# Projection groups in another order: index rows and softmax values first, queries and keys second, with the indexer inside the second group

## The reference

```python
a = rmsnorm(h, g_attn)
qa, ka, va, qi, ki, wi, qb, kb, vb, u = split_columns(a @ w_in)
qa = rope(rmsnorm(qa.reshape(B, T, 6, 64), g_q_a), pos)
ka = rope(rmsnorm(ka.reshape(B, T, 2, 64), g_k_a), pos)
qi = rope(qi.reshape(B, T, 4, 64), pos)
ki = rope(ki[:, :, None, :], pos)[:, :, 0]
...
s_idx = einsum('bqhd,bsd->bqhs', qi, ki) * 64 ** -0.5
score = einsum('bqhs,bqh->bqs', relu(s_idx), wi)      # the indexer
_, sel = top_k(where(causal, score, -inf), topk)      # 128 of 512 keys
...                                                   # softmax attention over sel
z = einsum('bqhd,bshd->bhqs', qb, kb) * 64 ** -0.5     # stick-breaking attention
rev = cumsum(where(strict, log_sigmoid(-z), 0), axis=3, reverse=True)
o_b = exp(where(strict, z + rev, -inf)) @ vb
```

## Time and profile before

| | |
|---|---|
| median of 3 runs | 1616.64 us (1613.22 to 1617.04) |
| the profiled execution, its own time | 1620.47 us |
| its span in the profile | 1618.7 us |
| PE busy | 1556.1 us, 96% |
| DVE busy | 883.4 us, 55% |
| ACT busy | 683.5 us, 42% |
| POOL busy | 276.4 us, 17% |
| mean granted TensorE clock | 0.984 of full speed |

### The profile page before, as it was taken

One profiled execution on the slowest core, in us unless ns is written; L12 is line 12 of the kernel. 1 busy time (PEld: TensorE's weight loads), 2 busy tenths in 40 slices (PEclk: granted clock), 3 DMA queues, 4 the chain that ended last, 5 costly groups with the idle time before them and its releaser, 6 DMA issues.

```text
span 1618.7 us, 30649 instructions
## 1 busy us (share of the span) xinstructions
PE 1556.1 (96%) x11772; PEld 1415.8 (87%) x11772; DVE 883.4 (55%) x1534; ACT 683.5 (42%) x995; POOL 276.4 (17%) x474
## 2 busy tenths in 40 slices
PE   6999989999999999999999998899999999999998
PEld 5787746999999999999977776479999999999998
DVE  6668884245555553222857688624455555432345
ACT  4444556244444442224443444644444444322241
POOL 3420340111111110100115105202111111101000
PEclk8999999999999999999999999999999999999999
DMA  5233144123333233322222511332233323333221
GB/s 166 66 99 87 34 142 110 53 66 91 91 90 89 80 87 100 92 81 85 79 69 77 138 40 58 105 98 86 72 91 91 91 78 91 98 88 92 84 70 61
DMA packets 225719, 140.24 MB, mean 87 GB/s; under 512 B 13122, under 2 KB 219604, under 8 KB 225552
## 3 DMA queue, kind: packets, MB, share of 16 engines
q1 hardware_dynamic: 223220, 133.46, 28.3%
q0 software_dynamic: 2400, 5.42, 1.0%
HBM read 131.21 MB, written 7.65 MB: 86 GB/s over the span
## 4 chain that ended last, share of the span: by engine, by line
PE 79%; DVE 13%; ACT 3%; issue 3%; POOL 1%; DMA 0%; DVEq 0%; SPq 0%; ACTq 0%; POOLq 0%
PE ps L1714 23%; PE ps L1716 22%; PE ps L1715 22%; DVE score L1379 3%; DVE m L1376 3%; DVE w_L L1270 2%; PE ps L2065 1%; PE ps L1994 1%; DVE Lb L1451 1%; PE ps L1741 1%; PE ps L1797 1%; PE ps L1905 1%; PE ps L1767 1%; PE ps L2149 1%; PE ps L1907 1%
## 5 line engine op out<-in xcount | busy, mean ns | idle before, releaser
L1714 PE MATMUL ps<-bH,w_H 128*128 128x272 f32 x1664 | 481.1, 289 | 4.7 <-DVE w_L L1270 3.2
L1270 DVE TENSOR_TENSOR w_L<-w_raw,w_H 128x1024 fp32r<-128x1024 f32 (+4 forms) x236 | 257.6, 1100 | 414.1 <-ACT w_H L890 411.3
L1716 PE MATMUL ps<-bH,w_L 128*128 128x272 f32 x1664 | 479.6, 288 | 0.0
L1715 PE MATMUL ps<-bL,w_H 128*128 128x272 f32 x1664 | 477.9, 287 | 0.0
L890 ACT ACTIVATE w_H<-w_raw 128x1024 fp32r<-128x1024 f32 (+4 forms) x236 | 220.1, 943 | 270.1 <-PE ps L1716 269.4
L1714 PEld LDWEIGHTS ps<-bH,w_H 128*128 128x128 f32 x1664 | 312.6, 188 | 6.3 <-DVE w_L L1270 4.1
L1715 PEld LDWEIGHTS ps<-bL,w_H 128*128 128x128 f32 x1664 | 313.6, 188 | 0.1
L1716 PEld LDWEIGHTS ps<-bH,w_L 128*128 128x128 f32 x1664 | 312.6, 188 | 0.0
L1714 PE MATMUL ps<-actH,w_H 128*128 128x272 f32 x704 | 204.2, 290 | 0.0
L1716 PE MATMUL ps<-actH,w_L 128*128 128x272 f32 x704 | 203.8, 289 | 0.0
L1715 PE MATMUL ps<-actL,w_H 128*128 128x272 f32 x704 | 202.7, 288 | 0.0
(11 more groups left out here) (343 smaller groups left out, 2326.6 us busy)
## 6 DMA issues: line engine op xcount, KB each, us to landing
w_raw<-in_w_up SPq DMA_DIRECT2D x88, 512.0 KB, 3.7
w_raw<-in_w_down SPq DMA_DIRECT2D x32, 512.0 KB, 3.9
w_raw<-in_w_in SPq DMA_DIRECT2D x24, 512.0 KB, 5.0
w_raw<-in_w_ple_gate SPq DMA_DIRECT2D x16, 512.0 KB, 3.9
w_raw<-in_w_down SPq DMA_DIRECT2D x16, 384.0 KB, 3.4
w_raw<-in_w_out SPq DMA_DIRECT2D x16, 320.0 KB, 3.5
w_raw<-in_w_in SPq DMA_DIRECT2D x8, 452.0 KB, 4.0
w_raw<-in_w_in SPq DMA_DIRECT2D x8, 384.0 KB, 3.6
```

Of the source, the lines that this page charges most:

```text
L1270: ins = dve.tensor_tensor(w_L[u % SPLIT][:, a:b], w_raw[raw_slot(l, u)][:, a:b], w_H[u % SPLIT][:, a:b].bitcast(F32), ALU.subtract)
L1714: pe.matmul(out, wh, xh, start=start, stop=False)
L1715: pe.matmul(out, wh, xl, start=False, stop=False)
L1716: return pe.matmul(out, wl, xh, start=False, stop=stop)
```

## The change

`CHUNK` is turned around: group 0 is now softmax values, index queries, key and weights (452 columns), group 1 the softmax queries and keys (512). All that hangs on the order of the groups follows: the index rows are rotated first (`rope_ok` 1 to 5) and the queries and keys last (`rope_ok` 6 to 10), and `turn(0, ...)` now has three blocks and `turn(1, ...)` four. The six calls of TensorE's `index` move from between the products of units 12 to 14 into group 1, after `k` 4, 5 and 6 and in the middle of `k` 5, 6 and 7; their banks change, and the first two tiles of group 2 wait for the last relus. Both parts of `decode_step` stand after `k` 5 (before: after 3 and after 5). GpSimd multiplies the gains into the rotation's tables once (`rot_q`, `rot_k`, each cos and sin for five tiles), so a tile needs one product on GpSimd instead of three; the squares are made by ScalarE (`ACT.Square` in `leave(1, t)`), and VectorE only adds them up. Seven of the 16 rounds for the first tile run before the rotations of queries and keys, six more between units 13 and 15, three after `split(16)`. From `select(2, 13, 16)` on the lists are as they were. SP's list isn't edited.

```diff
-CHUNK = [(0, 512), (512, 964), (1732, 2116)]
+CHUNK = [(512, 964), (0, 512), (1732, 2116)]
...
-CH_BLOCKS = [(F_QA, 4), (F_QI, 3)]
+CH_BLOCKS = [(F_QI, 3), (F_QA, 4)]
...
-                pool.tensor_scalar(gains[:, 0, :], gains[:, 0, :], 0.125, None, ALU.mult)
-                pool.wait_ge(hs_rec, at(hs_rec, 1))
+                pool.tensor_scalar(gains[:, 0, :], gains[:, 0, :], 0.125, None, ALU.mult).then_inc(pool_step, steps.step())
...
+                for g, out in ((0, rot_q), (1, rot_k)):
+                    gn = gains[:, g, :].unsqueeze(1)
+                    cs, sn = (dcon[:, d:d + TILES * HD].rearrange("p (t d) -> p t d", d=HD) for d in (D_COS, D_SIN))
+                    pool.tensor_tensor(out[:, 0, :, :], cs, gn.to_broadcast([P, TILES, HD]), ALU.mult)
+                    for a in (0, 32):
+                        pool.tensor_tensor(out[:, 1, :, a:a + 32], sn[:, :, a:a + 32],
+                                           gn[:, :, 32 - a:64 - a].to_broadcast([P, TILES, 32]), ALU.mult)
...
+                pool.wait_ge(hs_rec, at(hs_rec, 1))
...
+                    pool.tensor_tensor(x, x, hstat[0:n, t, :].unsqueeze(2).to_broadcast([n, 8, HD]), ALU.mult).then_inc(qk_ok, 1)
...
                 part_copy(0)
-                for t in range(TILES):
+                leave(0, 0)
+                split(5)
+                for t in range(1, TILES):
                     leave(0, t)
...
                 split(6)
+                turned(0, 0)
+                turned(0, 1)
+                turned(0, 2)
                 split(7)
...
+                turned(0, 3)
+                turned(0, 4)
+                relu(1, 0, 4)
                 split(8)
                 part_copy(1)
...
+                relu(2, 0, 4)
+                relu(3, 0, 4)
+                leave(1, 0)
+                leave(1, 1)
                 split(9)
...
                 split(10)
-                turned(0, 4)
-                turned(1, 0)
+                act.wait_ge(hs_ss, at(hs_ss, 5))
+                inverse(hstat[:, :, :], hstat[:, :, :], 1.0 / HD).then_inc(hs_rec, 1)
                 split(11)
...
+                turned(1, 4)
+                split(16)
...
+                select(1, 4, 7)
+                split(11)
                 qk(0)
-                split(7)
                 qk(1)
-                split(8)
+                split(12)
                 qk(2)
                 qk(3)
-                split(9)
+                split(13)
                 qk(4)
...
                     if step:
-                        pe.wait_ge(w_lo, at(w_lo, RAW + 4 * c + 3 + 1))
+                        u = 4 * c + 3
+                        pe.wait_ge(w_ld[raw_slot(l, u)], ld_value(l, u))
...
+                            if c == 1 and t == 1:
+                                if k in (2, 4):
+                                    turn(0, 1 if k == 2 else 4)
+                                elif k > 4:
+                                    index(k - 4, 2)
-                        if k in (3, 5):
-                            decode_step(c, (k - 3) // 2)
+                        if k == 5:
+                            decode_step(c, 0)
+                            decode_step(c, 1)
...
+                        if c == 1 and k in (1, 2, 3):
+                            turn(0, (0, 2, 3)[k - 1])
+                        if c == 1 and k in (4, 5, 6):
+                            index(k - 3, 0)
+                turn(1, 0)
...
-                for t in range(1, 4):
+                for n in range(3):
                     for half in range(2):
-                        feature(t - 1, half, 0, 4)
...
+                        feature(n, half)
+                        if 2 * n + half < 4:
+                            turn(1, 2 * n + half + 1)
```

More of the change, by code:

```diff
@@ L382, in build @@
         F_BANK = [1, 3, 5, 6, 6, 6, 6, 6]
[L383 removed]
+        I_BANK = [3, 4]
         def act_at(of, f):
@@ L732, in _ @@
-                    pool.tensor_tensor(x[:, 6:8, :], x[:, 6:8, :], gains[0:n, 1, :].unsqueeze(1).to_broadcast([n, 2, HD]), ALU.mult).then_inc(qk_ok, 1)
-                for t in range(TILES):
+                    store("a_v", t, "n d", V[:, t, 0:128], kv_out)
                     pool.wait_ge(rope_ok, at(rope_ok, t + 1))
                     hold(pool)
[L736 to L742, removed]
@@ L743, in _ @@
                     store("idx_k", t, "d", r_tok[:, t, 256:320], ix_out)
[L744 to L747, removed]
                 for t in range(1, 4):
@@ L753, in _ @@
                                        pattern=[[-1, P]], channel_multiplier=1).then_inc(i_diag, 1)
+                pool.wait_ge(hs_rec, at(hs_rec, 1))
+                hold(pool)
+                for t in range(TILES):
+                    n = TOKW[t]
+                    pool.wait_ge(p_ev, at(p_ev, 5 + t + 1))
+                    x = x_tok[0:n, t, :].rearrange("p (h d) -> p h d", d=HD)
+                    pool.tensor_tensor(x, x, hstat[0:n, t, :].unsqueeze(2).to_broadcast([n, 8, HD]), ALU.mult).then_inc(qk_ok, 1)
+                for t in range(TILES):
+                    pool.wait_ge(rope_ok, at(rope_ok, 5 + t + 1))
+                    hold(pool)
+                    store("a_k", t, "n d", r_tok[:, t, 384:512], ak_out)
+                    pool.wait_ge(p_ev, at(p_ev, 10 + t + 1))
+                    hold(pool)
+                    store("b_v", t, "n d", V[:, t, 128:512], kv_out)
                 pool.memset(qim, 0.0).then_inc(d_zero, 1)
@@ L970, in leave @@
                             act.wait_ge(n_rec, at(n_rec, 1))
-                        ins = copy(x_tok[0:n, t, :], src, r)
+                        copy(V[0:n, t, 0:128], src[:, 0:128], r)
+                        ins = copy(x_tok[0:n, t, 0:324], src[:, 128:452], r)
                     elif c == 1:
-                        copy(V[0:n, t, 0:128], src[:, 0:128], r)
-                        act.wait_ge(rope_ok, at(rope_ok, t + 1))
-                        ins = copy(x_tok[0:n, t, 0:324], src[:, 128:452], r)
+                        act.wait_ge(rope_ok, at(rope_ok, 5 if t == 0 else t + 1))
+                        if t >= 2:
+                            act.wait_ge(hs_ss, at(hs_ss, t - 1))
+                        copy(x_tok[0:n, t, :], src, r)
+                        ins = act.activation((t1, t2)[t % 2][0:n, :], src, ACT.Square, scale=r)
                     else:
@@ L1027, in _ @@
                     leave(2, t)
-                for t in range(1, 4):
-                    relu(t, 0, 4)
-                    split(U_F + t + 1)
+                turned(1, 0)
+                turned(1, 1)
+                split(14)
+                turned(1, 2)
+                turned(1, 3)
+                split(15)
+                turned(1, 4)
+                split(16)
                 def stick_exp(h):
@@ L1341, in qk @@
                     dve.wait_ge(qk_ok, at(qk_ok, t + 1))
+                    dve.wait_ge(t_mm, at(t_mm, t + 1))
+                    dve.wait_ge(ix_out, at(ix_out, 5 * 16))
+                    hold(dve)
                     rotate(t, 8, [(r_tok[0:n, t, 0:384], 0, 384, True), (r_tok[0:n, t, 384:512], 384, 512, False)])
@@ L1831, in _ @@
                             square_sum(0)
-                        if c == 1 and k == 1:
+                        if c == 1 and k == 0:
                             pe.wait_ge(lay_ld, at(lay_ld, 6 * 16))
@@ L1868, in feature @@
                         mm.then_inc(w_used, 1)
-                for t in range(1, 4):
+                for n in range(3):
                     for half in range(2):
-                        feature(t - 1, half, 0, 4)
-                        if t > 1:
-                            index(t, 2 * half)
-                        elif half:
-                            index(1, 0)
-                        feature(t - 1, half, 4, KD)
-                    if t == 1:
-                        index(1, 2)
+                        feature(n, half)
+                        if 2 * n + half < 4:
+                            turn(1, 2 * n + half + 1)
                 def logits(q):
```

132 lines of the change are left out of this document (57 added, 75 removed).

## The result

| | before | after |
|---|---|---|
| median | 1616.84 us (4 runs, 1613.22 to 1617.38) | 1644.12 us (4 runs, 1643.49 to 1645.89) |
| ratio, 95% interval | | 1.0165 (1.0149 to 1.0182) |
| profiled execution, its span | 1620.47, 1618.7 us | 1644.15, 1642.4 us |
| mean granted clock | 0.984 | 0.979 |

The account below looks back on a forecast made before the run. TensorE, busy 96% of the span, was taken as the bound. Per layer 9.6 (later remainders) + 2.7 (clock) - 1.5 (fewer rounds) = 10.8, 21.6 for both; added to the 1616.6 median: 1638 us, range 1623 to 1648.

Parts of the forecast that it names:

- the mechanism: Later last rotation delays unit 16's load, so TensorE stands 11 us ahead of its first remainders; chance 0.60.
- Rival C: More waits among group 1's index calls make rotations and all behind 3 us later: +28 us, 1644; chance 0.09.
- the ladder: Group 1's chain of index call, relu, weighing and index call again: twelve rungs, each between k blocks of 2.8 us.
- Ahead of the logits: TensorE's stretch through unit 12, predicted to start at 107.6, up to the stick-breaking logits, predicted at 130.3.
- the lead of 1 us: TensorE reaching the stick-breaking logits at 130.3 instead of 131.32, with indexer products moved ahead of unit 12.
- Group 1: Old 2.93 us decode_step wait goes, a new 2.4 us one comes ahead of index(2, 2), halving the clock; net -0.5 us.
- rival B: Same late load, cheaper: group 1's pause keeps full clock, rotations earlier, no clock loss after the long pause; 1624 to 1629; chance 0.20.
- The old wait's cause: The 2.93 us in group 1: splits of units 6 and 7 stood behind rotations sharing time with GpSimd.
- The load: rope_ok is 10 at 115.0, 10.9 us later; unit 16 issues 20.8 us after, at 135.8, and lands at 139.7.
- Behind the load: After unit 16's splits, five VectorE rounds take 6.8 us to stick_max; first remainders at 150.3 against 140.73.
- The clock: Behind the long pause ahead of the first remainders, TensorE runs 5.4 us at half clock, losing 2.7 us.
- Behind that: After the half-clock stretch, seven fewer first-tile rounds behind split(16) relieve VectorE, removing a TensorE wait: -1.5 us.

Follow-up runs that it names:

- e1: Changed kernel, with SP loading units 16 and 17 ahead of the wait for the last rotation and the index-key pages: 1617.74 us, ratio 1.0009.
- e3: Kernel before, with SP also waiting, ahead of the index-key pages, until VectorE has copied out unit 12's product: 1633.24 us, ratio 1.0099.
- e5: Kernel before, with SP loading units 16 and 17 ahead of the wait for the last rotation: 1618.52 us, ratio 1.0002.
- e11: e6 with VectorE's split(12) moved between the first and second rotation of queries and keys: 1608.06 us, ratio 0.9944 to the kernel before.
- e6: e1 with the two parts of decode_step back after k 3 and k 5: 1611.24 us, ratio 0.9957 to the kernel before.
- e9: Kernel before, with only the tables rot_q and rot_k, so GpSimd has one product per tile instead of three: 1611.05 us, ratio 0.9963.
- e10: Kernel before, with only the second part of decode_step waiting on the landed load instead of VectorE's split: 1612.81 us, ratio 0.9970.
- e4: Changed kernel, with 45 extra bf16 products keeping TensorE busy in the pause ahead of the first remainders: 1641.60 us, ratio 1.0150 to the kernel before.
- e7: e1 with ScalarE's relu(2, 0, 2) ahead of split(8) and relu(2, 2, 4) behind part_copy(1): 1616.54 us, ratio 0.9991 to the kernel before.
- e12: Kernel before, with both the rotation tables and the second decode_step part's wait on the landed load: 1610.63 us, ratio 0.9954.

## Why the prediction was right, step by step

The forecast (1638, range 1623 to 1648, slower) named the mechanism, and e1, e3 and e5 show it. The measured time is 6 us above it: 2 us are in the table below, and 4 us come from the baseline, since the profiled execution of before lies above its median and that of the change doesn't. Rival C, more waits inside group 1, had named 1644, the very time measured, but its mechanism didn't come: in group 1 there is one wait, the one of the forecast, and e1 gives the time back without touching the ladder.

- **Ahead of the logits.** Logits predicted at 130.3, measured 130.52; but TensorE's first dense product also started 0.85 us earlier, so the lead of 1 us didn't come in layer 0. Two errors cancelled: unit 12 started at 108.9, not 107.6 (a wait of 1.54 that I had set at nothing, because `split(12)` stands behind two rotations, as e11 shows on e6, where 1.21 of it were left), and the stretch behind it was 1.1 us shorter, for a reason that wasn't looked for. That the logits came on the forecast is luck. Nor did group 0 stay without a new wait: TensorE stood there for 1.31 us in layer 0, on VectorE's split. I had looked only at GpSimd's tables there, and their first product starts at 33.99, later than this wait. TensorE came sooner, at 33.0, since the group is narrower and one decode part no longer stands ahead, and VectorE's split began at 32.99, behind the same `aL` work as before:

```profile
34.29 0.44 PE L1731 MATMUL ps<-w_H,aH 128*128 128x452 f32 x1 [1.31 <-DVE w_L L1284]
```

- **Group 1.** The new wait of 2.4 us ahead of `index(2, 2)`, worked out link by link, came at 2.42 (2.65 in layer 1), and e6 shows its chain from `decode_step` to the load of unit 8. The clock behind it was wrong for layer 0: it stayed at 1.00. That part of rival B held there. The old wait's cause was right but named by half: e9 shows GpSimd's part, and e10 that the wait on a split, where a landed load is enough, was the other.
- **The load.** `rope_ok` 10 at 116.9 instead of 115.0: VectorE's `split(12)` ended at 108.9, not 107, because `split(11)` took 2.55 us and the first product of the first rotation 1.39 beside GpSimd, which scales there now (97.6 to 103.6). The 20.8 us to unit 16 came at 20.0, the landing at 140.9 instead of 139.7. ScalarE stood for 17 us, not 10, since it was free at 124, not 129: off the path, and it cost nothing.
- **Behind the load.** Split and rounds as worked out: 6.77 us against 6.8 from the split's end to `stick_max`. Remainders at 151.4 instead of 150.3.
- **The clock.** 4.4 us at half and 2.2 us lost (e4), against 5.4 and 2.7. The Trainium skill, "TensorE: Matmul & The Clock Gate", section "Part 1: The HAM clock gate", would have idling bring the lower clock and work release it; e4, where filling the pause keeps the clock up, agrees.
- **Behind that.** -1.5 was too much: from the third remainders to the fifth the change wins 0.8 us, and a new wait of 1.0 us stands ahead of the softmax logits, on VectorE's `u_tok` copies, which I hadn't looked at.

The whole account, from profile to profile (us, after less before, from the starts of TensorE's rows; "third" and "fifth" are the remainders of heads 2 and 4):

| stretch | predicted, a layer | layer 0 | layer 1 |
|---|---|---|---|
| up to the logits | -1.0 | -0.8 | -1.0 |
| logits to first remainders | +10.6 | +11.5 | +11.4 |
| first to third remainders (the clock) | +2.7 | +2.1 | +2.2 |
| third to fifth, and the rest of the layer | -1.5 | -0.8 and -1.6 | -0.8 and +1.5 |
| sum | +10.8 | +10.4 | +13.3 |

The rest of the layer has the same lists in both kernels, but stretches at half clock fall otherwise there. By windows of 1 us, the rest of the two layers has about 13.6 and 17.1 us of them before, and 6.8 and 20.5 now. At half a microsecond lost for each, an estimate, that is -3.4 and +1.7: the signs of the -1.6 and the +1.5, not their exact size. Why the clock falls in other places isn't known. The 23.7 us of the table and the 3.6 by which the profiled execution of before lies above its median make the 27.3 us of the result.

## What to carry to other kernels

A wait in an in-order queue holds everything behind it, also what doesn't need it. Before work is moved that such a wait stands on, measure from the semaphore to the load behind it (here 20.8 us), and the margin of that load (1.2 us, in no table of waits, since nobody waited yet); the last rotation moved by 12.8 us (104.1 to 116.9), ten times that. The cheap repair is to put the urgent loads ahead of the wait. And if a change brings nothing as a whole, try its small parts alone: two of them, a table made once and a wait on the load instead of the split, won 0.3 to 0.4% each without the new order (together 0.5%, since both take away the same wait).

## What was not expected of the hardware

The clock after a short pause does not follow from the length of the pause alone. In one execution of e3 the same wait came in both layers, 2.92 and 2.91 us long, and these are the stretches behind it:

```profile
73.10:79.90 6.80, 5.98 (x22) 4.12 (x23) 6.77 (x9) 1.85 (x4) 6.42 (x8) 0.51 0.38 115
873.30:879.90 6.60, 6.60 (x37) 5.05 (x38) 6.57 (x9) 1.86 (x4) 5.67 (x7) 1.00 0.42 130
```

Of the 14 waits of 2.42 to 3.01 us in group 1 of before, after and e1 to e5, ten were followed by 3.4 or 6.8 us at half the clock and four by none; of those of 0.9 to 1.95 us there (e7, e9, e10, e12) none was. What decides between the four and the ten stays open. It is a few us in either direction that the sums here couldn't name ahead.
